# Two modulation halves moved ahead of the third and fourth piece of an output projection

## The reference

```python
mod = cond @ mod_w[layer] + mod_b[layer]                 # six vectors of 1024
sh1, sc1, g1, sh2, sc2, g2 = split(mod, 6)
h = rms_norm(x, mix_norm_g[layer]) * (1 + sc1) + sh1
x = x + g1 * odd_mixer(h, ...)                           # layer 1
h = rms_norm(x, ffn_norm_g[layer]) * (1 + sc2) + sh2
x = x + g2 * moe(h, ...)                                 # 16 experts, two per token

def odd_mixer(h, ...):
    y_branch, x_branch = split(h @ in_w, 2)
    xc = causal_dwconv(x_branch, conv_w, conv_b)
    ...
    return (gelu(y_branch) * hseq) @ out_w
```

## Time and profile before

| | |
|---|---|
| median of 3 runs | 1945.02 us (1941.83 to 1945.78) |
| the profiled execution | 1945.16 us |
| its span | 1943.3 us |
| mean granted clock of TensorE | 0.975 of full speed |
| busy: TensorE, VectorE, ScalarE, GpSimd | 96%, 69%, 57%, 3% of the span |
| HBM read | 454.09 MB |

### The profile page before, as it was taken

The page is one execution under the profiler, slowest core; times in us unless marked ns, Lnnn a source line. Parts: engine busy times, 40 slices in busy tenths (PEclk is TensorE's granted clock), DMA queues, the critical chain, the costliest instruction groups (busy, mean ns, idle before and its releaser), DMA issues.

```text
span 1943.3 us, 27022 instructions
## 1 busy us (share of the span) xinstructions
PE 1863.9 (96%) x11125; PEld 1596.8 (82%) x11125; DVE 1346.6 (69%) x1756; ACT 1098.8 (57%) x1463; POOL 51.3 (3%) x54
## 2 busy tenths in 40 slices
PE   6988899999999899999999999999999999999998
PEld 4845788888778788888799987799989998789997
DVE  3786788888777688888856565566566555656655
ACT  4443677777658577777654446654445444655443
POOL 0000011000000010000000000000000000000000
PEclk9989899999999899999999999999999999989999
DMA  9767599999967589999945565355555556425551
GB/s 362 245 241 278 207 317 335 342 335 326 335 233 278 216 324 327 340 340 325 334 136 191 195 195 169 108 174 195 195 183 186 193 191 196 157 94 181 186 192 48
DMA packets 209322, 456.98 MB, mean 235 GB/s; under 512 B 8848, under 2 KB 20776, under 8 KB 209192
## 3 DMA queue, kind: packets, MB, share of 16 engines
q1 hardware_dynamic: 206416, 451.74, 66.5%
q10 hardware_dynamic: 2776, 3.43, 0.5%
HBM read 454.09 MB, written 1.05 MB: 234 GB/s over the span
## 4 chain that ended last, share of the span: by engine, by line
PE 90%; DVE 4%; ACT 3%; issue 1%; DMA 1%; SPq 1%; POOL 0%; ACTq 0%; DVEq 0%; POOLq 0%
PE bank L308 88%; PE bank L1990 2%; DVE rest L650 1%; PE bank L2265 1%; DMA raw<-in_mod_w 1%; SPq L593 1%; DVE arena L1246 1%; DVE arena L1238 0%; ACT round L633 0%; ACT hTh L799 0%; ACT arena L765 0%; ACT arena L1127 0%; DVE htokl L1238 0%; DVE xres L1238 0%; DVE hTl L1238 0%
## 5 line engine op out<-in xcount | busy, mean ns | idle before, releaser
L650 DVE TENSOR_TENSOR rest<-raw,round 128x1024 fp32r<-128x1024 f32 (+1 forms) x760 | 888.5, 1218 | 256.9 <-ACT round L633 256.5
L633 ACT ACTIVATE round<-raw 128x1024 fp32r<-128x1024 f32 (+1 forms) x760 | 759.2, 1050 | 404.1 <-PE bank L308 387.9
L308 PE MATMUL bank<-hTh,round 128*128 128x256 f32 x1600 | 449.3, 281 | 11.6 <-DVE hTl L1246 3.9
L308 PE MATMUL bank<-hTl,round 128*128 128x256 f32 x1600 | 446.7, 279 | 0.0
L308 PE MATMUL bank<-hTh,rest 128*128 128x256 f32 x1600 | 446.5, 279 | 0.0
L308 PEld LDWEIGHTS bank<-hTh,round 128*128 128x128 f32 x1600 | 304.1, 190 | 16.9 <-issue 10.8
L308 PEld LDWEIGHTS bank<-hTl,round 128*128 128x128 f32 x1600 | 305.1, 191 | 1.2 <-issue 0.5
L308 PEld LDWEIGHTS bank<-hTh,rest 128*128 128x128 f32 x1600 | 303.9, 190 | 0.0
L308 PE MATMUL bank<-round,hTh 128*128 128x512 f32 x464 | 186.3, 402 | 7.2 <-DVE hTl L1238 2.9
L308 PE MATMUL bank<-round,hTl 128*128 128x512 f32 x464 | 182.6, 394 | 0.0
L308 PE MATMUL bank<-rest,hTh 128*128 128x512 f32 x464 | 181.6, 391 | 0.0
(11 more groups left out here) (221 smaller groups left out, 2169.6 us busy)
## 6 DMA issues: line engine op xcount, KB each, us to landing
raw<-in_ex_w SPq DMA_DIRECT2D x192, 1024.0 KB, 5.4
raw<-in_mod_w SPq DMA_DIRECT2D x48, 1024.0 KB, 7.5
raw<-in_ffn_w_gate SPq DMA_DIRECT2D x44, 1024.0 KB, 5.0
raw<-in_ffn_w_up SPq DMA_DIRECT2D x44, 1024.0 KB, 5.1
raw<-in_ffn_w_down SPq DMA_DIRECT2D x44, 1024.0 KB, 4.8
raw<-in_w_in SPq DMA_DIRECT2D x20, 1024.0 KB, 5.1
raw<-in_ev_in_w SPq DMA_DIRECT2D x10, 1024.0 KB, 13.0
raw<-in_od_in_w SPq DMA_DIRECT2D x8, 1024.0 KB, 5.7
```

What stands on the lines that cost most here:

```text
L308: return e.matmul(o, l, r, start=start, stop=stop, skip_group_check=True)
L633: e.activation(hi[:, h], raw[:, h], ACT.Copy).then_inc(S("hi"), 1)
L650: e.tensor_tensor(lo[:, h], raw[:, h], hi[:, h].bitcast(F32), ALU.subtract).then_inc(S("lo"), 1)
```

## The change

Halves 22 and 23 go from behind the fourth out piece to between the second and the third, alike in the plan (DMA order), in ScalarE's list and in TensorE's. In the plan their four pieces come two out pieces earlier, and the third and the fourth out piece four positions later.

```diff
@@ weight_plan, odd()
         mod_two(21)
         out(0, 0)
         out(0, 1)
+        for q in LAST_MODS:
+            mod_two(q)
         out(512, 0)
         out(512, 1)
-        for q in LAST_MODS:
-            mod_two(q)
@@ act_program, odd()
                 act_split(e, ahead, out[1])
+                for q in LAST_MODS:
+                    mod_copy(e, q, copy)
                 act_split(e, ahead, out[2])
                 act_only(e, ahead, out[3])
                 norm_x(3)
-                for q in LAST_MODS:
-                    mod_copy(e, q, copy)
                 norm_h(3, False)
```

## The result

The changed kernel takes 1959.08 us against 1945.64 us for the kernel before (medians of 14 runs each, 13.4 us apart); the ratio of the runs, with their scatter taken in, is 1.0058, 95% interval 1.0043 to 1.0074, that is 11.3 us slower (8.4 to 14.4). Forecast were 9.9 us, or 1955.0 us with a range of 1950.5 to 1958.5. By the ratio, 1945.1 us become 1956.4 us, inside that range; the median by itself lies 0.6 us above its upper end. The profiled execution has a span of 1958.2 us. Single executions of one kernel differ by 10 us and more here (1938.51 to 1949.0 for before, 1947.2 to 1962.91 for the changed one), so that what follows reads the stretch itself in each profile and sets the times beside it.

What follows compares the result with a forecast made beforehand. TensorE, which ends the chain for 90%, was taken as the bound. Terms 3.64 + 2.90 + 1.6 + 1.9 - 0.1 = +9.9 us on 1945.1 gave 1955.0 us, range 1950.5 to 1958.5.

Steps and rivals of the forecast that it cites:

- The halves leave the shadow: 32 matmuls leave the 5.67 us shadow of residual, squares and root, so the fourth out piece ends 3.64 us later.
- A DMA slot carries other content: SP's issue times stay, contents change: the third out piece moves from position 2 to 6, landing at 618.3, not 607.1.
- Who waits for it: ScalarE's rounding of the third out piece waits, delaying half 21's copy and TensorE's eight small sums by 2.90 us.
- The clock after that wait: After about 2.8 us of idle at the sums, TensorE's clock falls to 1.2 GHz, costing 1.6 us.
- rival one: The wait at the sums comes but the clock holds through it: +8.3, 1953.4 us; chance 0.18.
- The clock at the norm: Idle ahead of the norm's transposes grows from 2.03 to 5.67 us and the clock falls there: 1.9 us.
- ScalarE's copies: Copies of halves 22 and 23 leave ScalarE's queue at the norm, between scaling and bank reads: -0.1 us.
- Rival two: The third out piece lands as a lone transfer, wait at the sums 0.3 us: +5.7, 1950.8 us; chance 0.10.
- Rival three: Behind the norm, the low clock phase moves into the idle and spares the router: +3.1, 1948.2 us; chance 0.04.
- Rival four: Low clock phases after both idles last twice as long (3.1 and 3.5 us): +13.0, 1958.1 us; chance 0.06.

Runs made afterwards that it cites:

- e2: Changed kernel with ScalarE's copy of half 21 ahead of the third out piece's rounding, plus 32 unused matmuls behind the fourth out piece; ratio 1.0014 to before.
- e6: Changed kernel with halves 22 and 23 between the third and fourth out piece instead, in all three lists; ratio 1.0041 to before.
- e4: Changed kernel with only half 22 moved, half 23 left behind the fourth out piece; ratio 1.0012 to before.
- e5: Changed kernel loading only the first quarter of each of the four pieces of halves 22 and 23 (256 KB, not 1 MB); ratio 1.0057 to before.
- e1: Changed kernel with ScalarE's copy of half 21 ahead of the rounding of the third out piece; ratio 1.0035 to before.
- e3: Kernel before, halves and plan unmoved, with ScalarE's copy of half 21 only behind the rounding of the fourth out piece; ratio 1.0050 to before.
- e12: Changed kernel unaltered, run once more for another profile; 1956.32 us beside 1955.21 for before, one run each.
- e11: Changed kernel with ScalarE's copy of half 21 first (as e1), and halves 22 and 23 on 8 of their 32 matmuls; ratio 1.0026 to before.
- e10: Kernel before, nothing moved, with halves 22 and 23 on only 8 of their 32 matmuls; ratio 0.9975 to before.

## Why the prediction was right

*The halves leave the shadow, 3.64 us.* Right: 3.9 us (e2 and e6 against before: 45.97 and 46.00 against 42.06; where the 0.3 us over the matmuls' own time come from stays open), 2.0 for one half (e4), and a filler in the old place is free (e2).

*A DMA slot carries other content.* Right in kind: position 6 was issued within 0.1 us of the time read before, and landed 8.2 us later where 7.6 was taken. e5 shows that the bytes ahead of it lengthen its transfer, and e6 that with the piece back at position 2 nobody waits. One reading was loose: the prediction gives as the reason for 7.6 us that positions 3 to 5 were still under way, but position 3, issued at 603.2, had landed 6.5 us later, at 609.7, before position 6 was issued at 610.7; only 4 and 5 were in flight. The Trainium skill, "DMA: Bandwidth & Descriptors", section "Anatomy of one DMA", has a fit for the path of GpSimd by which 1 MB would take an estimated 4.4 us. That is for a transfer by itself; issued by SP with nothing ahead of it one took 5.0 us, and the third out piece, behind others, 7.2 and 8.2. The measurement decides.

*Who waits for it: the copy of half 21 and, with it, TensorE, 2.90 us.* Right, by e1 and, with no DMA in it, e3. In the pair of profiles the idle was 3.32 us, 0.4 more, from the landing; in e12 2.33.

*The clock after that wait, 1.6 us.* What remains of 9.10 after 3.9 and 3.3 is 1.9 us, with 3.3 us at the low level in the rows. The clock fell in all three kernels that had an idle of over 2 us there (3.32, 2.33, and 4.56 in e3), and in none of the others with 0 to 1.1 us, so that rival one did not occur. The argument for the fall was weaker than its outcome: the prediction calls 2.80 us the shortest idle that was followed by the low clock, but the transposes of layer 0 ran low after 2.04 us, and the stretch at 593.40 after 1.86:

```profile
593.41 0.58 PE L308 MATMUL bank<-hTh,round 128*128 128x256 f32 x1 [1.86 <-ACT arena L1047]
```

*The clock at the norm, 1.9 us, and ScalarE's copies, -0.1.* The pair of profiles shows 2.33. But this term rested on one row of layer 0 against one of layer 1, taken as the price of a length of idle. Those two rows have the same idle (2.04 and 2.03 us), so they could not price its length. With the idle unchanged the same code gives anything from 20.0 to 24.6 us, and the difference of the means is 1.4 us, not clear of the scatter. That 1.9 came out near 2.33 is luck in good part: e12, the same kernel, has 22.19 us, e6 and e11, with the same idle, have 25.73.

*Rival two* (lands alone) is excluded by the landing; e5 comes near to it with less to load ahead. *Rival three* did not occur: the router stretch had low phases again (658.6 to 662 and 665 to 673 us). *Rival four* was near: in e6 and e11 the low phase lasted through the whole norm and router, 25.73 us.

The sum, 9.9 us, against 11.4 in the stretch of the profiles and 11.3 in the times: a little low in the landing, in the halves and in both clock terms of this execution. In e12 the same stretch is 76.29 us, 8.3 over before. So the mechanism up to the residual was right and is shown by e1, e3 and e6; the agreement of the sum within 1.5 us is in part the luck of the executions.

## What to carry to other kernels

In a weight stream in order, moving work moves its DMAs, and what slips back in the stream lands behind what moved up. Look for whoever rounds or copies that piece on another engine, and for what stands behind it in that engine's queue: here an innocent copy, in front of which one call too many cost more than the moved matmuls (5.2 us against 3.9). Work that fills the shadow of a latency chain is free where it stands (e2), and cost its full time in both of the other places tried; and a clock term read from a single pair of rows needs its spread, which the unchanged stretches of the same profiles give for nothing.

## What was not expected of the hardware

Modulation halves on 8 matmuls of 128x512 took 3.62 us, on 32 in four strips 3.64. The Trainium skill, "TensorEngine Tiling (Array Packing)", section "Theoretical Speedup", gives up to four times the throughput for a dimension of 32 or less; the trace agrees (3.62 against 3.64 us for four times the matmuls). The granted clock does not follow from the length of the idle just before: after 2.0 us the transposes ran at either level, after 3.75 us at the high one, after 5.6 us always at the low one (six of six). And a low phase can be free: where it was shorter by 3 us after the start of the y projection's second half, TensorE arrived 1.2 to 1.6 us earlier and, in the old order, waited 0.8 us of that for ScalarE; the residual of e10 comes only 0.07 us sooner than that of before (41.99 against 42.06).
